# Summing the two experts of a pair inside TensorE's accumulation instead of in two VectorE adds

## What is computed

```
g = softmax(cv)                                                    # 8 heads x 16 experts for each token
hid = gelu(einsum('bd,bhkd->bhk', xb, u_tab[eid]))
return einsum('bhk,bhkd->bd', g * hid, v_tab[eid])                 # added to x
```

## Time and profile before

| | |
|---|---|
| median of 3 executions | 2469.34 us (2468.39 to 2471.63) |
| the profiled execution | 2471.63 us |
| its span, first to last instruction | 2469.9 us |
| TensorE busy | 1690.5 us |
| VectorE busy | 1601.3 us |
| mean granted TensorE clock | 0.783 of full |

### The profile page before, as it was taken

How to read it: one execution, slowest core, us unless ns; L and a number is a source line. 1 busy time by engine, 2 the same in 40 slices (tenths; PEclk the granted TensorE clock), 3 DMA queues, 4 the chain that set the end, 5 groups by cost and what they waited for, 6 DMA issues and landing times.

```text
span 2469.9 us, 31173 instructions
## 1 busy us (share of the span) xinstructions
PE 1690.5 (68%) x10696; PEld 1166.6 (47%) x10696; DVE 1601.3 (65%) x4243; ACT 798.3 (32%) x1761; POOL 688.0 (28%) x608
## 2 busy tenths in 40 slices
PE   8989848477899638956788636747799863333333
PEld 7889827235786307734667304623678630000000
DVE  3381157867755676878765566787675577777774
ACT  2122143232263325232445224322226232233221
POOL 0000032213222333323233242121322244444442
PEclk9999969688899759977889757868889875555555
DMA  7666799789899999999999999978989999999996
GB/s 263 219 234 223 269 367 413 295 351 394 321 394 392 384 422 408 420 422 388 382 370 420 421 422 416 373 296 344 378 312 402 360 393 421 421 422 422 421 417 280
DMA packets 127837, 905.89 MB, mean 367 GB/s; under 512 B 16112, under 2 KB 16576, under 8 KB 18368
## 3 DMA queue, kind: packets, MB, share of 16 engines
q0 software_dynamic: 82944, 604.02, 59.9%
q1 hardware_dynamic: 44736, 299.90, 31.0%
HBM read 895.75 MB, written 8.11 MB: 366 GB/s over the span
## 4 chain that ended last, share of the span: by engine, by line
PE 38%; DMA 23%; DVE 23%; ACT 7%; issue 4%; DVEq 3%; POOL 2%; POOLq 0%; ACTq 0%
PE bank L1078 20%; DMA uv<-uv_in,idx_u 19%; DVE uv L986 9%; PE bank L1084 8%; PE bank L1381 5%; DVE yB L685 4%; ACT L424 3%; DMA ring<-w_in 2%; DMA ring<-cache_in 2%; POOL uv L361 2%; ACT diag L630 1%; DVEq L680 1%; DVE tmp_s L695 1%; DVE yB L700 1%; DVE x L1007 1%
## 5 line engine op out<-in xcount | busy, mean ns | idle before, releaser
L361 POOL DMA_INDIRECT uv<-uv_in,idx_u x576 | 645.6, 1121 | 1588.9 <-PE bank L1381 1207.8
L986 DVE CUSTOM_DVE_ANT_0 uv<-uv,xrep 128x1024 f32<-128x1024 f32 x576 | 683.0, 1225 | 213.2 <-DMA uv<-uv_in,idx_u 212.8
L1381 PE MATMUL bank<-uv,diag 128*32 128x512 f32 x2304 | 446.7, 851 | 523.8 <-ACT diag L630 523.0
L1078 PEld LDWEIGHTS bank<-xnT,ring 128*128 128x128 f32 x4096 | 551.0, 202 | 114.1 <-issue 104.3
L1078 PE MATMUL bank<-xnT,ring 128*128 128x128 f32 (+1 forms) x4096 | 576.4, 301 | 30.8 <-ACT yMA L424 17.0
L1381 PEld LDWEIGHTS bank<-uv,diag 128*32 128x32 f32 x2304 | 57.6, 126 | 775.6 <-ACT diag L630 713.7
L424 ACT ACTIVATE pick<-pick 128x2 f32<-128x2 f32 (+1 forms) x324 | 69.8, 216 | 1051.8 <-DVE pick L986 1051.1
L424 ACT ACT_TABLE_LOAD x255 | 327.2, 1283 | 12.8 <-DMA x<-x_in 4.6
L685 DVE SCALAR_TENSOR_TENSOR yB<-ext_p,small,yB 128x128 f32<-128x128 f32 x960 | 283.0, 357 | 20.4 <-issue 1.4
L630 ACT ACTIVATE diag<-gated_fold,pick 128x32 f32<-128x32 f32 x576 | 154.2, 315 | 9.5 <-ACT pick L424 0.2
L1078 PE MATMUL bank<-yMA,ring 128*128 128x128 f32 (+1 forms) x1024 | 142.1, 293 | 7.8 <-DVE merged L865 7.8
(11 more groups left out here) (152 smaller groups left out, 1534.7 us busy)
## 6 DMA issues: line engine op xcount, KB each, us to landing
ring<-w_in SPq DMA_DIRECT2D x224, 1024.0 KB
ring<-cache_in SPq DMA_DIRECT2D x32, 1024.0 KB
uv<-uv_in,idx_u POOLq DMA_INDIRECT x576
phase<-rows_in SPq DMA_DIRECT2D x4, 1024.0 KB, 6.9
ring<-keys_in SPq DMA_DIRECT2D x4, 1024.0 KB
ext_s<-state_in SPq DMA_DIRECT2D x2, 1088.0 KB, 11.1
convs_out<-ext_s SPq DMA_DIRECT2D x2, 1088.0 KB, 26.6
ext_s<-mem_in SPq DMA_DIRECT2D x2, 1024.0 KB, 14.2
```

The source lines that it names most:

```text
L361: nc.gpsimd.indirect_dma_start(out=uvbuf[2 * b + i], out_offset=None, in_=uv_in, in_offset=bass.IndirectOffsetOnAxis(ap=ids[:, c:c + 1], a ...
L986: ins = V.tensor_tensor_reduce(out=u, in0=u, in1=xrep[gg % 2][:, :], scale=1.0, scalar=0.0, op0=ALU.mult, op1=ALU.add, accum_out=hid[:, c: ...
L1078: ins = MM(out, w[:, k, P * b:P * (b + 1)], rhs(k), start=k == 0, stop=k == KB - 1)
L1381: ins = MM(vbank[gg % 2][c:c + 32, :], diag[:, t % 4, i], uvbuf[2 * b + i][:, D + 512 * n:D + 512 * (n + 1)], start=first, stop=last)
```

## The change

The two matmuls of a half `n` (expert `i` = 0 and `i` = 1) now write the same 32-partition strip, `n`, and accumulate there. The first of a group starts the sum only for `i` = 0, and the last closes it only for `i` = 1. Strips 2 and 3 of the banks are no longer used. `add_group` has two adds and no drain in place of four adds and one drain. Number, shapes and order of the matmuls, the gathers, the waits and all else stay.

```diff
             def add_group(gg):
                 m, t, _, r0 = GROUP[gg]
                 dve.wait_ge(S["v_used"], 2 * PAIRS * (gg + 1))
-                for i in range(2):
-                    if i:
-                        dve.drain()
-                    for n in range(2):
-                        xs = x[r0:r0 + 32, t, 512 * n:512 * (n + 1)]
-                        ins = V.tensor_tensor(xs, xs, vbank[gg % 2][32 * (2 * i + n):32 * (2 * i + n + 1), :], ALU.add)
+                for n in range(2):
+                    xs = x[r0:r0 + 32, t, 512 * n:512 * (n + 1)]
+                    ins = V.tensor_tensor(xs, xs, vbank[gg % 2][32 * n:32 * (n + 1), :], ALU.add)
                 ins.then_inc(S["xadd"], 1)
...
                 for i in range(2):
                     for n in range(2):
-                        c = 32 * (2 * i + n)
-                        ins = MM(vbank[gg % 2][c:c + 32, :], diag[:, t % 4, i], uvbuf[2 * b + i][:, D + 512 * n:D + 512 * (n + 1)],
-                                 start=first, stop=last)
+                        ins = MM(vbank[gg % 2][32 * n:32 * (n + 1), :], diag[:, t % 4, i], uvbuf[2 * b + i][:, D + 512 * n:D + 512 * (n + 1)],
+                                 start=first and i == 0, stop=last and i == 1)
                 ins.then_inc(S["v_used"], 1)
```

## The result

The changed kernel takes 2491.35 us (median of 4, 2488.98 to 2492.54) against 2468.86 us of the kernel before: ratio 1.0087, 95% interval 1.0070 to 1.0102, so 17 to 25 us slower. Run again on another chip it gave 1.0070 (1.0051 to 1.0089). I had forecast 59 us. The time lies inside my range of 2480 to 2578, near its lower end. The sign and the cost of a single pair on TensorE were right; what the pairs together do to the time was not.

A forecast was written before the change was run, and what follows sets the result against it. No engine alone bounds it: gather bandwidth without mixing; TensorE, VectorE and transfers by turns in mixing stretches. 49 + 9 + 15 + 1.7 (last pair) - 12 - 4 = +58.7 us, forecast 2528 us, range 2480 to 2578.

The forecast's parts named there:

- What a pair costs: A pair's value matmuls on TensorE, two deep: +0.86 us at the high clock, +1.70 at the low one.
- First and third stretch, +49: Mixing stretches 330 to 815 and 1500 to 2010 us: 56.8 us of L1381 on the chain, times 0.87, +49 us.
- Second stretch, +9: Mixing stretch 915 to 1395 us, DMA share 0.98: half of 18.4 us counted, +9 us.
- Off-chain pairs, +15: Mixing-stretch pairs not on the chain: many have room, an eighth of 119 us charged, +15 us.
- the clock, -12: 15 low-clock chain pairs in mixing stretches: busier TensorE gets the high clock sooner, half of 25.5 us returned, -12 us.
- small loss by the clock: Rival: TensorE reaches high clock in all 15 low-clock pairs and matmuls around them, 2475 to 2486 us; chance 0.07.
- Stretches without mixing, 0: 815 to 915, around 1395 to 1500, 2010 to end: the queue of gathers covers longer pairs, 0 us.
- The adds, -4: VectorE's group sums: 36 of 72 adds and 18 drains go, -4 us, bounds 0 and -24.6.

The follow-up runs named there:

- the 48 pairs: Kernel before plus four zero-weight matmuls behind value matmuls of the 48 chain pairs in the first and third mixing stretches: 1.0153, +38 us.
- All 61 pairs together: Kernel before plus four zero-weight matmuls behind the value matmuls of every pair 66 to 126, the second mixing stretch: 0.9992, -2 us.
- experiment 4: Kernel before plus four zero-weight matmuls behind the value matmuls of the 98 mixing-stretch pairs not on the chain: 0.9957, -11 us.
- the 65 chain pairs: Kernel before plus four zero-weight matmuls behind the value matmuls of the 65 mixing-stretch pairs on the chain: 1.0121, +30 us.
- experiments 5 and 6: Kernel before plus zero-weight matmuls for the 98 off-chain pairs, placed after `v_used` is raised (0.9971, -7 us) or ahead of the diag wait (0.9953, -12 us).
- experiment 15: Kernel before plus zero-weight matmuls ahead of the diag wait, only for the 53 off-chain pairs of first and third mixing stretches: 0.9989, -3 us.

## Why the prediction was off, step by step

- **What a pair costs** (+0.86 and +1.70): right. +0.84 measured in a dense passage and +1.58 at the low clock; L1376 busy +264.6 us. Strips run beside each other, and depth costs in full.
- **First and third stretch, +49**: right in kind, somewhat too large; the 48 pairs measured +38, with what the clock gave back already in it. I multiplied every us that the chain had of L1381, also beside waits for weight tiles; that some of it is taken up there is my reading, and no run shows it.
- **Second stretch, +9**: wrong, and the more plainly as I had its DMA share of 0.98 in hand. All 61 pairs together measured -2. I halved a cost that the row said was covered.
- **Off-chain pairs, +15, and the clock, -12: the step that failed.** I took the off-chain pairs for a cost and priced the clock only in the 15 low-clock pairs on the chain. Measured, the 98 off-chain pairs are -11 where I had +15: 26 of the 36 us that are missing. The example that I gave for their room, the pair at 545.71 us, is itself on the chain (pair 21, one of the 65): idle time ahead of a pair is no room if the chain comes through the diag matrices that it waits for. Of the off-chain pairs only a third have idle time just ahead of them. What they do gain is on the matmuls around them: with fillers there and nowhere else, TensorE's other work shrank by some 28 us, at a higher granted clock, and in the changed kernel by 47. One part of that was open to see: the "small loss by the clock" rival had the mechanism, at a chance of 0.07. The Trainium skill ("TensorE: Matmul & The Clock Gate", Part 1) states that activity releases the throttle; the profile agrees, the same two records taking 0.49 us after and 0.80 before, and the granted clock of the mixing stretches rising with every filler or longer pair put into all three (0.85 or 0.86 before, 0.87 to 0.89 in experiment 4, 0.89 to 0.92 after).
- **The price of that rival** does not follow from its own terms. +70 less 25 for the pairs and 15 for the matmuls around them is +30, not +5 to +15; at 2499 us it would have stood inside the forecast and nearer to the result than its centre.
- **Stretches without mixing, 0**: right, 1.0000 measured, though clock and busy time there changed much.
- **The adds, -4**: right beside two-deep strips (3 to 5 for the second two), too small alone (11).

The sum with measured terms: 38 (48 chain pairs) - 11 (98 off-chain pairs) + 0 (no mixing) - 4 (adds) = +23, for a measured +22 and +17. It leaves out the 17 chain pairs of the second stretch, at about nothing by the traces. The agreement is partly luck: with the +30 that the 65 chain pairs measured in place of 38 the sum is +15, and with 11 for the adds it is lower still. The terms are known to some 5 us each.

What stays open: how the 11 us of the off-chain pairs are spread over the stretches. In the traces of experiments 5 and 6 the first part (pair 0 to 60) is no shorter than before (551.9 and 552.1 us for 551.2), the second 3.5 and 2.5 us shorter and the third 5.2 in both; but the two halves alone gave 3 and 2, and the trace of experiment 15 has no gain in the third (531.0 for 530.5). A clock that carries over from one passage to the next, or a chain that moves when only half of it is relieved, would both do that, and no run here separates them. That the clock is the cause of the 11 us is shown only so far: fillers win at each of three places around these pairs, the granted clock rises, and other matmuls get shorter by 20 us or more. No run held the clock fixed.

None of the kernels that keep the output is much better than the kernel before; the one with fillers ahead of the wait for diag (0.9953) beats both.

## What to carry to other kernels

Packing matmuls into separate column strips makes them run beside each other; accumulating them in one strip to save an add moves time from a rare VectorE instruction to every matmul, here 0.84 us at the high clock and 1.58 at the low one for each of 288 pairs, to save 36 adds of 0.68. Cost an edit by stretch. Where a stretch's transfers are already at full share, added work on an engine with idle time left may cost nothing, until that time is used up: here one filler a pair cost 0 and three cost 46 us. And before calling added TensorE work a cost, look at the granted clock around it: behind pairs off the chain it paid for itself here, behind pairs on the chain it didn't.

## What the hardware showed that I had not expected

- Useless matmuls with zero weights beside pairs off the chain made the kernel 0.3 to 0.5% faster (0.9957, 0.9971, 0.9953), with the other matmuls' busy time at 1216, 1211 and 1224 us, and at 1244 to 1256 without them.
- A second dose raised the mean clock further (0.797 to 0.817) and lost the gain again (0.9994).
- Fillers in the stretches without mixing raised their granted clock from 0.52 to 0.73 and TensorE's busy time from 168 to 250 of 447 us, with no effect on the time.
